# A hybrid decoder layer on one core: rows kept with features on partitions, norms applied behind the products

## The reference, cut to what matters

```python
def rmsnorm(x, g):
    return x * lax.rsqrt(jnp.mean(x * x, axis=-1, keepdims=True) + EPS) * g

hn = rmsnorm(h, g_attn_norm)                  # norm 1; h is (2048, 1024), fp32
z = hn @ w_in                                 # q 512, k 128, v 128, u 512 columns
q = rmsnorm(q per head, g_q); k = rmsnorm(k per head, g_k)
a = sliding_window_sink_attention(q, k, v, attn_sinks, rel_bias)   # window 128
m = multiscale_pool_mixer(u, w_pool, pool_scale)                   # trailing means minus u
h = h + concat(a, m) @ w_out
hn = rmsnorm(h, g_ffn_norm)                   # norm 2
h = h + (silu(hn @ w_gate) * (hn @ w_up)) @ w_down                 # D_FF = 2816
gate = sigmoid(rmsnorm(h, g_ple_norm) @ w_ple_gate)                # norm 3
h = h + gate * (p @ w_ple_proj)               # p is (2048, 256)
```

## Time and profile before

| | |
|---|---|
| runs | 2092.46, 2086.13, 2092.34 us; median 2092.34 |
| profiled execution | span 2083.8 us, from its first to its last instruction |
| busy share of the span | PE 98%, DVE 65%, ACT 44%, POOL 15% |
| granted TensorE clock | 0.998 of full over the span |
| DMA | 295.41 MB, 142 GB/s over the span |
| TensorE by slice of 52 us | 7 tenths in the first, 9 in all others but the last, 8 |

### The profile page before, as it was taken

The page is one execution under the profiler, slowest core; times in us unless marked ns, Lnnn a source line. Parts: engine busy times, 40 slices in busy tenths (PEclk is TensorE's granted clock), DMA queues, the critical chain, the costliest instruction groups (busy, mean ns, idle before and its releaser), DMA issues.

```text
span 2083.8 us, 26814 instructions
## 1 busy us (share of the span) xinstructions
PE 2046.8 (98%) x9866; PEld 1697.3 (81%) x9866; DVE 1347.3 (65%) x1895; ACT 917.7 (44%) x1517; POOL 317.3 (15%) x501
## 2 busy tenths in 40 slices
PE   7999999999999999999999999999999999999998
PEld 6877788887788888888888888888888888888887
DVE  3676654657586565565788754966556566987653
ACT  4485663667553333333333543533333333333632
POOL 2343435544210000000000100000000000000100
PEclk9999999999999999999999999999999999999999
DMA  7667566573972322323916027632232328352143
GB/s 194 201 183 237 182 205 215 163 239 117 305 222 66 92 86 71 106 71 135 336 44 192 21 61 219 170 106 71 72 106 66 94 84 292 138 163 70 42 131 101
DMA packets 211998, 295.41 MB, mean 142 GB/s; under 512 B 15883, under 2 KB 135604, under 8 KB 210588
## 3 DMA queue, kind: packets, MB, share of 16 engines
q1 hardware_dynamic: 186848, 212.97, 33.6%
q0 software_dynamic: 23040, 79.23, 11.4%
q10 hardware_dynamic: 1980, 1.50, 0.3%
HBM read 226.51 MB, written 68.69 MB: 142 GB/s over the span
## 4 chain that ended last, share of the span: by engine, by line
PE 89%; DVE 3%; ACT 3%; DMA 2%; issue 2%; SPq 0%; POOL 0%; DVEq 0%; ACTq 0%; POOLq 0%
PE bank L2516 13%; PE bank L2518 13%; PE bank L2520 13%; PE bank L2204 7%; PE bank L2206 7%; PE bank L2205 7%; PE bank L2578 7%; PE bank L2580 7%; PE bank L2579 7%; PE bank L2232 2%; DMA raw<-in_w_in 1%; PE bank L2221 1%; PE bank L2223 1%; PE bank L2222 1%; PE bank L2264 1%
## 5 line engine op out<-in xcount | busy, mean ns | idle before, releaser
L2516 PE MATMUL bank<-a_hi,ring_hi 128*128 128x512 f32 x1232 | 480.3, 390 | 0.7 <-issue 0.7
L2520 PE MATMUL bank<-a_hi,ring_lo 128*128 128x512 f32 x1232 | 479.4, 389 | 0.0
L2518 PE MATMUL bank<-a_lo,ring_hi 128*128 128x512 f32 x1232 | 479.3, 389 | 0.0
L2516 PEld LDWEIGHTS bank<-a_hi,ring_hi 128*128 128x128 f32 x1232 | 231.3, 188 | 49.5 <-issue 1.3
L2520 PEld LDWEIGHTS bank<-a_hi,ring_lo 128*128 128x128 f32 x1232 | 231.3, 188 | 47.9
L2518 PEld LDWEIGHTS bank<-a_lo,ring_hi 128*128 128x128 f32 x1232 | 231.3, 188 | 47.8
L2578 PE MATMUL bank<-d_hi 128*128 128x512 f32 x616 | 240.8, 391 | 0.0
L2580 PE MATMUL bank<-d_hi,d_lo 128*128 128x512 f32 x616 | 239.8, 389 | 0.0
L2579 PE MATMUL bank<-d_lo,d_hi 128*128 128x512 f32 x616 | 239.7, 389 | 0.0
L1338 ACT ACTIVATE d_hi<-keep 128x1024 fp32r<-128x1024 f32 x132 | 139.8, 1061 | 201.5 <-PE bank L2580 184.4
L1933 DVE TENSOR_TENSOR d_lo<-keep,d_hi 128x1024 fp32r<-128x1024 f32 x132 | 161.1, 1223 | 50.9 <-ACT d_hi L1338 50.5
(11 more groups left out here) (255 smaller groups left out, 3924.4 us busy)
## 6 DMA issues: line engine op xcount, KB each, us to landing
w_parts<-w_split POOLq DMA_DIRECT2D x88, 512.0 KB, 4.9
hidden_T<-hid POOLq DMA_DIRECT2D x88, 256.0 KB, 2.3
raws<-in_w_gate SPq DMA_DIRECT2D x84, 256.0 KB, 4.7
raws<-in_w_up SPq DMA_DIRECT2D x84, 256.0 KB, 5.1
keep<-hidden_T SPq DMA_DIRECT2D x66, 256.0 KB, 3.7
raw<-in_w_ple_gate SPq DMA_DIRECT2D x64, 256.0 KB, 4.2
keep<-in_w_down SPq DMA_DIRECT2D x44, 256.0 KB, 4.3
other<-hidden_T SPq DMA_DIRECT2D x44, 256.0 KB, 6.8
```

Source lines behind the costliest of these rows:

```text
L2516: mm(dst[:, :], wh[:, g, cols], a_hi[o][:, k, :], start=fresh and k == 0, stop=False, skip_group_check=True)
L2518: mm(dst[:, :], wh[:, g, cols], a_lo[o][:, k, :], start=False, stop=False, skip_group_check=True)
L2520: ins = mm(dst[:, :], wl[:, g, cols], a_hi[o][:, k, :], start=False, stop=k == 3, skip_group_check=True)
```

## The change

x, p and the output are handed over with features on partitions (turned outside the kernel), the gains as columns; h, h1, the FFN's input, the projection and the staged rows are kept so too. Every product except kv and q now has the weights stationary. A norm's scaling is applied after the squares are summed over partitions: ACT squares a chunk, POOL adds the chunks into `acc`, TensorE turns `acc` (`turn_squares`), DVE reduces it (`sum_squares`), POOL makes rstd. Norm 1 is not applied ahead: the products take x times the gain, and q, kv and u are scaled when they leave their banks; for u, and for norms 2 and 3 (where DVE scales chunks in `scale_pair`), rstd is turned into a row broadcast over partitions (`turn_rstd`, ACT `spread`).

```diff
+Z_ORDER = {0: (2, 3, 4, 5, 0, 1, 6, 7, 8, 9)}     # z(0): the q panels first, kv at places 4 and 5
-N1_AT, N2_AT, N2_BANK, N2_SQUARES_AT, N2_SCALE_AT, N2_LAST_AT, N2_IN_FFN
+CHUNK_AT = {2 + k: k for k in range(8)}
+SUM1_AT, SPREAD1_AT = 13, 12
+SQUARES2_AT = {0: (0, 1), 1: (2, 3), 2: (4, 5), 3: (6, 7)}
+SUM2_AT, SPREAD2_AT = 6, 11
+SCALE2_AT = {13: 0, 14: 1, 15: 2, 16: 3}
+SQUARES2_LAST_AT = {0: (0, 1, 2, 3), 1: (4, 5, 6, 7)}
+SUM2_LAST_AT, SPREAD2_LAST_AT = 4, 6
+SCALE2_LAST_AT = {7: (0, 1), 8: (2,), 9: (3,)}
+SQUARES2_OF_LAST_AT = {8: 0, 9: 1, 10: 2, 11: 3}
...
 @block.gpsimd
+def add_squares(n, j, slots, into):
+    pool.wait_ge(sq_done, 8 * n + j + 1)
+    if j > 1:
+        pool.wait_ge(acc_done, 7 * n + j - 1)
+    elif n:
+        pool.wait_ge(acc_T, n)
+    nc.gpsimd.tensor_tensor(into[:, :], slots[:, 0, :] if j == 1 else into[:, :], slots[:, j % 2, :],
+                            ALU.add).then_inc(acc_done, 1)
...
 z_section(t), each half:
+    if t == 0 and half < 8:
+        for j in {0: (1,), 2: (2, 3), 4: (4, 5), 6: (6, 7)}.get(half, ()):
+            add_squares(NORM1[0], j, sq, acc)
+        if half == 7:
+            powers(NORM1[0])
+    if t == 0 and 8 <= half < 15:
+        add_squares(NORM1[1], half - 7, sq, acc)
+    if t == 0 and half == 10:
+        build_bias()       # the DMAs of the bias table, with their waits; before: ahead of z(0)
+    if t == 0 and half == 18:
+        powers(NORM1[1])
...
 @block.scalar
+def square(n, j, src, slots):
+    if j >= 2:
+        act.wait_ge(acc_done, 7 * n + max(j - 2, 1))
+    elif n:
+        act.wait_ge(acc_done, 7 * n - 1 + j)
+    nc.scalar.activation(slots[:, j % 2, :], src, ACT.Square).then_inc(sq_done, 1)
+def spread(n, psum, dst):
+    act.wait_ge(rstd_T, n + 1)
+    nc.scalar.activation(dst[:, :], psum[:, :], ACT.Copy).then_inc(spread_done, 1)
+def norm_hi(src, k):
+    nc.scalar.activation(wide_hi[:, k, :], src, ACT.Copy,
+                         scale=gains[:, 0, k:k + 1]).then_inc(nhi, 1)
...
 down_section, ple_section (ACT):
-        if k in (5, 6):
-            squares_late(g, 2 * k - 10)
-            squares_late(g, 2 * k - 9)
+        if -6 <= k < -2:
+            square_late(g, k + 6)
+        if k == 5:
+            for j in (4, 5, 6):
+                square_late(g, j)
+        if k == 6:
+            square_late(g, 7)
-        if k == 9:
-            norm3_hi(g, 0)
-    for b in range(1, NB):
+    spread(NORM3[g], bank[BS1[1]], spread3)
+    for b in range(NB):
         norm3_hi(g, b)
...
-        for b in range(NB):
-            squares_late(g + 1, b)
+        for j in range(KC):
+            square_late(g + 1, j)
     split(ple + 2)
...
 @block.vector
+def sum_squares(n, psum):
+    dve.wait_ge(acc_T, n + 1)
+    nc.vector.tensor_reduce(out=ssum[:, n, :], in_=psum[:, :].rearrange("p (b d) -> p b d", b=NB),
+                            axis=AX.X, op=ALU.add).then_inc(summed, 1)
+def scale_pair(out, src, gain, k0, by, signal):
+    for i in range(2):
+        ins = nc.vector.scalar_tensor_tensor(out=out[:, i, :], in0=src[:, k0 + i, :],
+                                             scalar=gains[:, gain, k0 + i:k0 + i + 1], in1=by[:, :], ...)
+    ins.then_inc(signal, 1)
+def copy_u(s, g):                      # before: on ACT, L1050
+    dve.wait_ge(panel_used, Z_AT[s] + 7 + g)
+    if s:
+        dve.wait_ge(u_carried, 4 * (s - 1) + g + 1)
+    dve.wait_ge(spread_done, NORM1[s] + 1)
+    nc.vector.tensor_tensor(u[:, g, CARRY:], bank[g][:, :], spread1[:, :], ALU.mult).then_inc(ucopied, 1)
...
 z_section(t), t = 0:
+    if half == 7:
+        sum_squares(NORM1[0], bank[4])
         constants()
+    if half == 8:
         dve.wait_ge(band_bank, 1)
+        nc.vector.tensor_copy(band[:, :], bank[7][0:NQ, 0:BAND]).then_inc(band_built, 1)
...
 down_section (DVE):
-        if k in (6, 7):
-            normalise3(g, k - 6)
         if k == 8:
-            p_lo_part(g, 0)
-            p_lo_part(g, 1)
-        if k == 9:
-            normalise3(g, 2)
-            norm3_lo(g, 0)
+            p_lo_part(g)
+            sum_squares(NORM3[g], bank[BS1[0]])
+    normalise3(g, 0)
+    normalise3(g, 1)
+    norm3_lo(g, 0)
+    normalise3(g, 2)
     norm3_lo(g, 1)
     normalise3(g, 3)
     norm3_lo(g, 2)
...
 @block.tensor
+def turn_squares(n, into, dst):
+    pe.wait_ge(acc_done, 7 * n + 7)
+    for b in range(NB):
+        ins = nc.tensor.transpose(dst[:, b * P:(b + 1) * P], into[:, b * P:(b + 1) * P], ident[:, :])
+    ins.then_inc(acc_T, 1)
+def turn_rstd(n, dst):
+    pe.wait_ge(rstd_done, n + 1)
+    for b in range(NB):
+        ins = nc.tensor.transpose(dst[:, b * P:(b + 1) * P],
+                                  rstd[:, n, b:b + 1].to_broadcast([P, P]), ident[:, :])
+    ins.then_inc(rstd_T, 1)
...
 down_step_of:
-        mm(dst, ah[:, tok], wh, start=fresh and k == 0, stop=False, skip_group_check=True)
-        mm(dst, ah[:, tok], wl, start=False, stop=False, skip_group_check=True)
-        ins = mm(dst, al[:, tok], wh, start=False, stop=k == FPAIRS - 1, skip_group_check=True)
+        mm(dst, wh[:, cols], ah, start=fresh and k == 0, stop=False, skip_group_check=True)
+        mm(dst, wh[:, cols], al, start=False, stop=False, skip_group_check=True)
+        ins = mm(dst, wl[:, cols], ah, start=False, stop=k == FPAIRS - 1, skip_group_check=True)
 ple_section: the first product of the first section waits spread_done (before: nlo of all of norm 3)
```

More of the change, by code:

```diff
@@ L932, in ffn_section @@
                 if half == 0:
-                    for b in range(NB):
-                        powers(NORM2[3], b)
+                    for k in range(4, KC):
+                        add_squares(NORM2[3], k, sq, acc)
+                    powers(NORM2[3])
                 for c in range(FPAIRS):
@@ L1752, in z_section @@
                         constants()
-                    if t == 0 and half == 6:
+                    if t == 0 and half == 8:
                         dve.wait_ge(band_bank, 1)
-                        nc.vector.tensor_copy(band[:, :], bank[4][0:NQ, 0:BAND]).then_inc(band_built, 1)
-                    if half in (2, 3):
-                        copy_kv(t, 2 * half - 4)
-                        copy_kv(t, 2 * half - 3)
-                    if t == 0 and half in (10, 11, 12, 13):
-                        scale_rows(NORM1[1], half - 10, x1[:, half - 10, :], x1[:, half - 10, :], g1)
@@ L1761, in z_section @@
-                    if t >= 2 and half in N2_SCALE_AT:
-                        normalise2(t - 2, N2_SCALE_AT[half])
+                        nc.vector.tensor_copy(band[:, :], bank[7][0:NQ, 0:BAND]).then_inc(band_built, 1)
+                    if t == 0 and half == 17:
+                        sum_squares(NORM1[1], bank[5])
+                    for b in COPY_KV_AT[t > 0].get(half, ()):
+                        copy_kv(t, b)
+                    if t >= 2 and half == SUM2_AT + 1:
+                        sum_squares(NORM2[t - 2], bank[6])
@@ L1763, in z_section @@
+                    if t >= 2 and half in SCALE2_AT:
+                        normalise2(t - 2, SCALE2_AT[half])
+                    for g in U_COPY_AT[t > 0].get(half, ()):
+                        copy_u(t, g)
                     if half in QK_MEAN_AT.get(t, {}):
@@ L2245, in transpose_q @@
                     pe.wait_ge(attn_sum, done)
+                if b == 1 and s in (1, 2):
+                    pe.wait_ge(summed, NORM1[s + 1] + 1)
                 for c in range(PAIRS):
@@ L2431, in z_section @@
+                    if half == SPREAD1_AT:
+                        pe.wait_ge(qcopied, 4 * t + 4)
+                        turn_rstd(NORM1[t], bank[3])
                     if t:
```

937 lines of the change are left out of this document (440 added, 497 removed).

## The result

The changed kernel takes 2151.28 us (median of 4 runs, 2149.25 to 2153.26), against 2092.12 for the kernel before on the same chip: ratio 1.0294 [1.0278, 1.0309]. The forecast was 2111.6, with a range up to 2126. The direction is right, the size is not. In the profiled executions the span went from 2083.8 to 2151.3 us, +67.5, where the prediction's sum has +19.3: 48.2 us are missing in it. That overstates the loss. In every run for which both are recorded the time is 1.8 to 2.2 us above the span of the same run, so the profile of before shows an execution near its fastest (2086.13), and the profile of after shows its slowest (2153.26). By the medians the change costs 59.2 us, and 39.9 are missing. The 8.5 us that the prediction adds to its span are for the most part the same spread, and not something that lies around the span.

What follows compares the result with a forecast made beforehand. TensorE, busy 98% of the span, was taken to bound the kernel: savings of 42.2 us and stalls of 61.5 gave +19.3 on the span of 2083.8, and 8.5 more for the median gave 2111.6 us, range 2072 to 2126.

Steps and rivals of the forecast that it cites:

- TensorE's work: Whole kernel: 98 transpose groups saved at 0.446 us, 24 added for norms, products unchanged in either role; net -33.0 us.
- The start: Before and in the first panels: first product near 10.8 us, second panel held back until near 18.8; -5.8 us.
- z(0): First z section: kv products wait for the band, +4.9 us; POOL's bias chain delays panel 9 in half 17, +13.0.
- u copies: z(t) to out(t): copy_u on DVE stands ahead of the rest of the pool step; +5.6 us over three transitions.
- DVE's longer lists: z(1) and z(3): DVE has 8 scalings of 512 columns for 4 of 1024; +1.0 and +1.5, together +2.5 us.
- out(3): out(3): eight ACT squares, chained to POOL adds from the third on, stand ahead of the attention steps; +3.6 us.
- out(0) and out(1): There seven POOL adds each precede the last qk squares, and qk_mean(3) precedes add_out; +1.1 and +1.8, together +2.9 us.
- FFN: First beats: four scale_pairs ahead of the last a_lo, +1.9 us; pair 1's weights issued behind four stores, +1.1; +3.0.
- Late halves: Both ple sections: sum 2.2, spread 0.9, DVE's scaling ahead of adds 5.1, panel splits 3.1 and 1.2; +25.0 us.
- sign (adds of 2 us): POOL: the prediction's account was to count as wrong if the adds of squares take 2 us, against 1.31 assumed.
- The third rival: POOL's adds take up to 2.1 us, not 1.3, beside DVE; 17 on TensorE's chain, +13.6 us, time 2125; chance 0.10.
- The first rival: Savings of 42.2 us come in full, waits on ACT, DVE and POOL mostly overlap, 17.3 remain; time 2067; chance 0.20.

Runs made afterwards that it cites:

- experiment 11: Changed kernel with DVE's pool_y_rest of groups 2 and 3 ahead of copy_u(3) in half 19 of z(1) to z(3): 2145.83 us, 1.0279 of the kernel before.
- experiment 4: Changed kernel with SP's x chunk loads one weight panel later in out(0) and h loads ahead of chunk loads in out(1): 2146.58 us, 1.0269 of the kernel before.
- experiment 7: Changed kernel with 60 extra products of 512 columns into an idle bank, in the gap of half 17 of z(0): 2147.36 us, 1.0272 of the kernel before.
- experiment 9: Changed kernel with POOL's adds from the third square on cut to 4 of 512 columns, most sums left out: 2127.59 us, 1.0192 of the kernel before.
- experiment 14: Kernel of experiment 13 with POOL's adds from the third square on cut to 4 of 512 columns: 2068.29 us, 0.9896 of the kernel before.
- experiment 1: Changed kernel with POOL's three bias table steps issued in halves 10, 11 and 18 of z(0), not all in 10: 2144.33 us, 1.0257 of the kernel before.
- experiment 2: Changed kernel with DVE's four adds of the FOURTH down product ahead of norm 3's scaling: 2152.92 us, 1.0301 of the kernel before.
- experiment 12: Changed kernel with three edits at the FFN's first beats, moving norm 2 scalings and the turn of rstd: 2149.53 us, 1.0295 of the kernel before.
- experiment 13: Changed kernel with order mended together in z(0), out sections, SP's queue, u copies, FFN beats and late halves: 2082.70 us, 0.9973 of the kernel before.

## Why the prediction was wrong

Step by step, in its own order.

- **TensorE's work, -33.0: right.** Counts, 0.45 us a group and the free exchange of roles; the trace leaves some 34.
- **The start: right in the first product** (10.01 us, forecast near 10.8), wrong behind, and its number is near by luck. Panel 1 was not held back; its lo began at 13.78. Instead the first products ran at half rate, 2.4 us, and some small waits followed; panel 2, which waited for its DMA until 21.43, cost 0.2 us of them.
- **z(0): right in cause, small in size.** kv 4.7 for 4.9, half 17 14.6 for 13.0. But behind these two gaps 2.0 and 1.2 us went at half rate, and more in the first panel.
- **u copies, 5.6: right** (1.9, of which 1.1 stood there before, + 2.35 + 2.35; experiment 11).
- **DVE's longer lists, 2.5, and out(3), 3.6: right in cause** where the trace has a gap for them (2.54 us at 462.61, 2.77 at 566.82). No experiment takes the first one alone.
- **out(0) and out(1), 2.9: undersized.** The h adds cost 3.0 and 3.9, and the 3.7 at 205 is missing. The prediction priced the order of a queue once, for the stores ahead of pair 1 in the FFN (1.1), but not for SP here: `load_chunk` waits for `norm_lo`, now later, and the weight panel waits behind it (experiment 4). With the half rate behind them these sections are 13 us above their terms; this is the largest miss of a place.
- **FFN, 3.0: undersized.** The three gaps there are 2.6, 3.5 and 4.1, with 1.4, 1.4 and 1.2 at half rate behind. The wait for rstd's turn was seen for norm 3 and not for norm 2.
- **Late halves, 25.0: right term by term.** 2.07, 1.05, 5.22, 2.75 and 1.85 us in the first, 2.07, 1.05, 5.21, 3.00 and 2.13 in the second, for 2.2, 0.9, 5.1, 3.1 and 1.2. 3.6 and 3.4 us of half rate behind the two large ones of each half come on top. The 3.1 for the panel behind eight squares was met by luck in part: 1.0 of the 2.75 and 3.00 is DVE's `w_lo` beside POOL's add, which the term does not have.

So the step that failed is the sum of the stalls, +61.5 less the 9.2 of the start, which prices each gap at its own length and leaves out gaps: the disturbed time grew by 101.5 us, not by 52.3. Most of its stalls are those of the trace, but three things have no term in it. First the half rate behind a gap: what products 0.43 us apart cost against 0.23 grew from 13.4 to 37.3 us, 24 of the missing 49 (experiment 7 shows what it hangs on; none of the earlier trace rows shows it, though the trace of before has two such stretches). Second the gaps in SP's queue and in the FFN. Third the adds on POOL: 1.31 us assumed, 1.51 measured in the mean. The mean hides two groups. 22 of all 84 adds took 1.80 to 3.16 us, and by the prediction's own sign (adds of 2 us) its account of POOL is wrong for these; most of the others took 1.3. The third rival's mechanism was thus there, at 0.5 to 0.8 more per add and once 1.9, but only in part where it named places: four slow adds are around the start of the FFN, none stands ahead of half 17 of z(0), and 14 are those of the first tokens in the late halves, where the gap stayed (2.07 us) when they were cut short in experiment 9. It also slowed DVE, 1.0 us ahead of the first gate panel in each late half. Experiments 9 and 14 put the full length of the adds, not only their excess, at 24 and 14 us. How much of that is the excess alone is not shown.

The first rival, absorption, did not come about in the change as made: the stalls left gaps, and most of the large ones a slow stretch behind them. And gaps do not simply subtract either: experiments 1, 2 and 12 took gaps away and got half, nothing and a third of them in their sections, since a second wait stood behind. Only after all of them were moved together did the savings of 42 us show (experiment 13), and then as 5 us. There the span is 5.1 us shorter than before, with 29.3 us more of disturbed time and some 35 us less of TensorE's own work. 16.2 of the 29.3 go with the short adds (experiment 14); the cause of the other 13.1 stays open.

The order of the new work and the clock behind it, not the layout, cost the 59 us: experiment 13 has the same 26129 instructions as the change as made and is 3% faster. The two accounts overlap, and their shares are not to be added: where the order leaves a chain in TensorE's way, the length of its adds is waited for as well.

## What to carry to other kernels

On an engine that is 98% busy, price a new gap of some microseconds at its length and the slow stretch that may follow (here 1.2 to 2.2 us behind most gaps of over 2.3), and list the waits of every queue that a moved step is put on, SP's among them. Before a gap is taken away, look up which wait ends next behind it; if it is the same producer, the gap only moves. A change that trades work of the busiest engine for a chain over three others has to be scheduled anew before it can be judged. And before a span is subtracted from another, look where its execution lies among the runs: here one near the fastest of its kernel stood against the slowest of the other, and 8 us of the difference were that.

## What was unexpected of the hardware

TensorE's clock fell to its level of 1.2 GHz after short pauses too. Behind gaps of 2.35 us at 334.33 and at 483.89, 1.2 and 1.6 us were lost; behind those of 2.07 at 1253.09 and 2011.43, nothing that the sum shows, and nothing behind 2.64 at 255.97. The loss varies between gaps of one length, and between executions at one place: the gap of 2.35 that is at 483.89 here is at 478.38 in experiment 7, which changes nothing near it, and there the products behind it ran 0.23 apart. In the start of z(0) 2.4 us went at half rate although TensorE was busy from 10.01 on.

POOL's adds of 128x512 took either 1.3 us or up to 3.2, by what DVE did. I compared all 84 with DVE's timeline. Of the 48 that meet no DVE tensor_tensor with both inputs in SBUF, 46 took 1.26 to 1.32 us, and two of 1.56 and 1.57 lie beside a scaling of DVE, which reads SBUF twice as well (seven more that meet one took 1.3). Of the 36 that meet one, 27 took 1.41 to 3.16. A short case: DVE's instruction runs from 22.52 to 23.75, the add begins at 23.09 and takes 1.81, which is the 0.66 left of it and 1.15 more. POOL, then DVE:

```profile
23.09 1.81 POOL L806 TENSOR_TENSOR acc<-acc,sq 128x512 f32<-128x512 f32 x1 [5.24 <-ACT sq L1036]
```

```profile
22.52 1.23 DVE L1530 TENSOR_TENSOR w_lo<-raw,w_hi 128x1024 fp32r<-128x1024 f32 x1 [4.13 <-ACT w_hi L1029]
```

Where the add began first, DVE paid instead: 2.22 us in place of 1.22 at 2040.24, while the add beside it took its usual 1.3. The longest case lengthened both. The durations by form (ns, least/median/most) and the row of that add; then DVE's row:

```profile
L806 POOL TENSOR_TENSOR acc<-acc,sq x72: 1262/1297/3156, 14.3 to 2040.1; 128x512 f32<-128x512 f32 x72
...
617.72 3.16 POOL L806 TENSOR_TENSOR acc<-acc,sq 128x512 f32<-128x512 f32 x1
```

```profile
616.37 3.35 DVE L1849 TENSOR_TENSOR a_lo<-a_raw,a_hi 128x2048 fp32r<-128x2048 f32 x1
```

The same DVE instruction takes 2283 ns in the mean where the adds are short (experiment 9). The Trainium skill ("SBUF — State Buffer", Who interferes with whom) has a VectorE instruction with two SBUF inputs and a GpSimd instruction that reads SBUF block each other for a whole instruction. The trace agrees, on either side, in the cases above; the median of 1297 ns says only that more than half of the adds met no such instruction.
